# Decode states of an SSD mixer: GpSimd multiplies by C, VectorE only sums

## The chip, the cores and the metric

The kernel runs on one core of a Trainium2 chip. The metric is device time in microseconds (us): the median over executions. The stretch that matters here lies between 120 and 236 us of a profiled execution of 605.8 us.

## What is computed

One layer of a hybrid decoder, in float32, for 256 prompt rows and 8 decode rows (one new token for each of 8 sequences). After one input projection, one half of the columns feeds a gated convolution of 31 taps, the other a state-space block (SSD) with 16 heads in 4 groups. Then come an output projection, a mixture of 16 experts in 4 groups, a gate and a last norm. The part that changes is the SSD step of the 8 decode rows:

```
def step(h, inp):                      # for the prompt, in 2 chunks of 128 rows
    dec, st = inp
    return dec[..., None, None] * h + st, h
...
h_t = exp(dt_t A) h_{t-1} + dt_t x_t B_t^T        # for each decode row: state 64 x 128 in each head
y_t = h_t C_t                                     # sum over the 128 columns of the state
y = y + d_skip[:, None] * xs
y = y * silu(z)
```

and the decode rows' own convolutions: `causal_dwconv` of 31 taps over 30 kept rows and the new one, and one of 4 taps over x, B and C.

## The kernel before

Tensors lie with features on the 128 partitions. `T` is 264 columns: 256 prompt columns and 8 decode columns. Each engine has its own program in order; semaphores join them.

TensorE (`pe`) projects 40 blocks of 128 columns through `project(n)`, 32 of them before the SSD part. Then it transposes x, B and the decode rows' B and C (`bc_psum`), and runs 8 items, `item(i)`: two chunks times four groups. After each item one more projection stands (the last two convolutions by matmul, `c6` and `c7`, and blocks of z). An item needs `m_ready` from VectorE: the decay matrix `mexp` times `cbm`.

VectorE's loop over the 8 items does, for item i: `difference(i + 1)` (4 `tensor_scalar`, L1366), `spread_done(i)` (L1330, and in the second chunk L1335 and L1336), `take(i)` (it takes the item's result out of PSUM: L1346, or L1349 and L1350, and L1353 twice), and from i = 2 on `decode(i - 2)`. Behind item 1 it also runs `decode_conv()`, the 31-tap convolution of the decode rows (L1245 multiplies 1984 columns, L1248 sums them, L1250 adds the bias).

The decode state has 8 pieces of 128 partitions x 8 rows x 128 columns (1024 columns). For piece i:

- ScalarE, `decode(i)`: 8 activations scale the old state in place (L686), 8 more make `outer`, that is dt x times B (L691). B lies spread over all partitions in `bbc`, two groups at a time, C in `cbc`.
- GpSimd, `new_states(i)`: adds the two (L464), stores the new state to HBM (L470), for some pieces loads a later old state into a free place (L469). Behind pieces 1 and 3 it issues the DMA that spreads the next group of B (`spread_b`, L507), behind pieces 4 and 6 that of C (`spread_c`, L511), since `cbc` comes free when VectorE has read it.
- VectorE, `decode(i)`: 8 instructions `tensor_tensor_reduce` (L1378 in the profile, each with a read of its accumulator) multiply the new state by C and sum; then one small `scalar_tensor_tensor` (L1383) adds d_skip times x and sets `y_s_ready`.

ScalarE's loop for item i: `exp_of(i + 1)`, `exp_carry(i + 1)` in the second chunk (L667, which waits for item i to be done), a spread, `decode(i)`, and the evacuation of the projection behind the item. Ahead of piece 6 it also runs Silu over z (L727).

After the loop VectorE multiplies y by z for four groups (`gate_y`, L1409): three of them, then `decode(6)`, `decode(7)`, and the last one. The output projection (L989) needs all four and the norm behind them. It is followed by the experts, whose weights stream from HBM.

The spreads of B and C may start once `bbc`'s place is free. That place is `glu`, which the SP queue reads in 64 DMAs (L369, 16 for each of the four convolutions by matmul).

Of the kernel before, what the change touches and what calls it, by code (L numbers as in the profile page):

```python
# [83 lines left out]
def build(nc, xT, pT, w_in, w_dt, w_out, w_moe, w_router, b_router, w_pleg, w_ple, params, hparams,  # L84
          conf_s, ssm_s, state_s, yT, conf_p_out, ssm_p_out, h_p_out, conf_s_out, ssm_s_out, h_s_out):
    with ExitStack() as ctx:
# [42 lines left out]
        outer = scratch[:, 8192:10240].rearrange("p (q b n) -> p q b n", q=2, b=NSM)  # L129
# [113 lines left out]
        ln_rs = sem("ln_rs")  # L243
# [28 lines left out]
        snew_ready = sem("snew_ready")  # L272
        y_s_ready = sem("y_s_ready")
# [3 lines left out]
        grs = sem("grs")  # L277
# [4 lines left out]
        out_conf, out_ssm, out_h_p, out_h_s, out_y = [sem("out_" + n) for n in ("conf", "ssm", "h_p", "h_s", "y")]  # L282
# [36 lines left out]
        z_ready = sem("z_ready")  # L319
# [16 lines left out]
        def _(sp):  # L336
# [47 lines left out]
            for j in range(MOER):  # L384
                s = MOE_SLOT[j]
                if s < MIXR:
                    read(last_user[s])
                elif s == 3:
                    sp.wait_ge(proj_ready, POS["c", 7, 0] + 1)
                elif s >= 9:  # L390
                    sp.wait_ge(ycat_ready, NG)
                    sp.wait_ge(out_conf, 32)
                    sp.wait_ge(y_s_ready, KD)
                elif s == 8:
                    sp.wait_ge(snew_ready, KD)
# [33 lines left out]
            for s, n in ((out_conf, 2), (out_ssm, 2), (out_h_p, 1), (out_h_s, KD)):  # L429
                sp.wait_ge(s, 16 * n)  # L430
# [3 lines left out]
        def _(pool):  # L434
# [49 lines left out]
            for j in range(KD):  # L484
# [95 lines left out]
        def _(act):  # L580
# [98 lines left out]
            def decode(i):  # L679
# [32 lines left out]
            act.wait_ge(bc_psum, 1)  # L712
            a.activation(bc_keep, ps[0:64, 2, 0:P], ACT.Copy).then_inc(rows_kept, 1)
            exp_of(0)
            spread(2)
            for i in range(2 * NG):
# [6 lines left out]
                if i == 6:  # L723
# [3 lines left out]
                    a.activation(z0, z0, ACT.Silu).then_inc(z_ready, 1)  # L727
# [104 lines left out]
        def _(pe):  # L832
# [99 lines left out]
            for c in range(2):  # L932
                if c == 1:
                    pe.wait_ge(xconv_done, NX // 2)
                for hf in range(2):
# [5 lines left out]
                    ins.then_inc(xtok_psum, 1)  # L941
            project(NFIRST + 2)
# [230 lines left out]
        def _(dve):  # L1173
# [131 lines left out]
            decode_conv_x()  # L1305

# [4 lines left out]
            dve.wait_ge(out_ssm, 32)  # L1311
# [58 lines left out]
            def decode(i):  # L1370

                dve.wait_ge(snew_ready, i + 1)
                dve.wait_ge(c_loaded[i // 2 % 2], 16 * (i // 4 + 1))
                at = [0, 0]
                for b in range(NSM):
                    if b > 1:
                        dve.wait_ge(dve_self, at[b % 2])
                    at[b % 2] = mark(v.tensor_tensor_reduce(  # L1378
                        out=pr_s[:, 256 + P * (b % 2):256 + P * (b % 2 + 1)], in0=state[:, i % STATES, b, :],
                        in1=cbc[:, i // 2 % 2, b, :], scale=1.0, scalar=0.0, op0=ALU.mult, op1=ALU.add,  # L1380
                        accum_out=cat[:, 8 + i, NPR + b:NPR + b + 1]))
                dve.wait_ge(dve_self, at[1])
# [8 lines left out]
            for i in range(2 * NG):  # L1391
# [6 lines left out]
                if i == 0:  # L1398
                    dve.wait_ge(out_ssm, 32)
                if i == 1:  # L1400
                    decode_conv()
# [11 lines left out]
            dve.wait_ge(z_ready, 1)  # L1413
# [283 lines left out]
```

## Time and profile before

| | us |
|---|---|
| median of 3 runs | 608.87 (606.99 to 611.69) |
| profiled execution, its own time | 607.55 |
| its span, first to last instruction | 605.8 |
| TensorE busy in the span | 542.8 (90%) |
| VectorE busy | 266.5 (44%) |
| ScalarE busy | 162.4 (27%) |
| GpSimd busy | 87.6 (14%) |

The span is the time from the first to the last instruction that the profiler recorded; the execution's own time is 1.75 us longer. Busy shares are means over stages with very different limits. From 175 to 213 us, the last six items, VectorE is busy 27.02 of 38 us, ScalarE 32.37, TensorE 30.36 and GpSimd 18.56.

### The profile page before, as it was taken

What the parts mean: (1) busy time and instruction counts of PE and PEld (TensorE: products, weight loads), DVE (VectorE), ACT (ScalarE), POOL (GpSimd) and SP (SyncE); (2) the same over time, 40 slices, a digit from 0 to 9 for tenths busy, and PEclk for the clock granted to TensorE, in tenths of its full rate; (3) what the DMA queues carried; (4) which work ended last, traced back from release to release, by engine and by line L of the source; (5) the groups of instructions that cost most, each with busy time, mean ns of one, the idle gap of its engine ahead of it and who ended that gap; (6) DMA issues with size and microseconds to landing.
All of it is one profiled execution on the core that took longest, in us unless ns stands there. A gap on an engine that the chain in (4) does not pass through costs nothing.

```text
span 605.8 us, 7656 instructions
## 1 busy us (share of the span) xinstructions
PE 542.8 (90%) x2743; PEld 350.4 (58%) x2743; DVE 266.5 (44%) x783; ACT 162.4 (27%) x381; POOL 87.6 (14%) x104
## 2 busy tenths in 40 slices
PE   5999999999757877999976899999999999999994
PEld 3788888877525665888762344434343434343782
DVE  1799789413587676102271040404040404040553
ACT  3211311132488783312241101010101111111543
POOL 4000166123144440030000000000000000000000
PEclk9999999999869887999997899999999999999997
DMA  8733444449767860277972999999999999999101
GB/s 340 248 139 141 143 153 163 136 52 268 226 222 251 281 225 27 83 257 294 425 288 72 413 400 398 423 419 422 422 421 421 422 420 421 420 422 421 70 0 71
DMA packets 35609, 164.18 MB, mean 271 GB/s; under 512 B 6440, under 2 KB 12920, under 8 KB 19200
## 3 DMA queue, kind: packets, MB, share of 16 engines
q1 hardware_dynamic: 24960, 139.69, 58.8%
q0 software_dynamic: 6080, 21.80, 10.3%
q10 hardware_dynamic: 4544, 2.37, 1.5%
q8 instruction: 14, 0.23, 0.2%
q14 instruction: 11, 0.09, 0.0%
HBM read 153.43 MB, written 8.26 MB: 267 GB/s over the span
## 4 chain that ended last, share of the span: by engine, by line
PE 64%; DMA 16%; DVE 8%; issue 4%; SPq 3%; ACT 3%; POOL 2%; POOLq 0%; DVEq 0%; ACTq 0%
PE ps L889 14%; DMA xbc<-u_rows,slot_tok 12%; PE ps L989 10%; PE ps L1138 10%; PE ps L1109 10%; PE ps L1164 5%; PE ps L1152 4%; SPq L369 3%; PE ps L1075 2%; DVE xraw_s L1378 2%; DMA ring<-glu 2%; POOL glu L489 2%; PE ps L880 1%; DVE mexp L1366 1%; DMA ring<-bc_rows 1%
## 5 line engine op out<-in xcount | busy, mean ns | idle before, releaser
L889 PE MATMUL ps<-u,ring 128*128 128x264 f32 x640 | 144.7, 388 | 0.9 <-issue 0.9
L889 PEld LDWEIGHTS ps<-u,ring 128*128 128x128 f32 x640 | 122.1, 191 | 22.5 <-issue 1.6
L1109 PE MATMUL ps<-ring,xraw 128*64 128x512 f32 x512 | 114.9, 601 | 1.2 <-ACT xraw L792 1.2
L1109 PEld LDWEIGHTS ps<-ring,xraw 128*64 128x64 f32 x512 | 35.7, 138 | 69.2 <-issue 69.0
L1583 DVE TENSOR_TENSOR h<-h,ps 128x264 f32<-128x264 f32 x64 | 27.5, 429 | 86.0 <-PE ps L1152 85.2
L989 PE MATMUL ps<-cat,ring 128*128 128x264 f32 x256 | 59.5, 395 | 1.6 <-DVE cat L1428 1.6
L1138 PE MATMUL ps<-ring,xraw 128*64 128x512 f32 x256 | 58.6, 611 | 0.0
L989 PEld LDWEIGHTS ps<-cat,ring 128*128 128x128 f32 x256 | 49.7, 195 | 11.5 <-issue 2.7
L563 POOL DMA_INDIRECT xbc<-u_rows,slot_tok x9 | 8.6, 954 | 271.1 <-DVE slot_tok L1542 219.8
L1138 PEld LDWEIGHTS ps<-ring,xraw 128*64 128x64 f32 x256 | 18.1, 141 | 35.1 <-issue 35.1
L489 POOL TENSOR_TENSOR glu<-asg 128x256 f32<-128x256 f32 x8 | 21.4, 2671 | 94.7 <-ACT asg L637 94.7
L1152 PE MATMUL ps<-glu,xraw 128*128 128x264 f32 x128 | 30.6, 392 | 0.0
L1577 DVE TENSOR_TENSOR xraw<-xraw,ps 128x512 f32<-128x512 f32 x8 | 5.5, 688 | 55.7 <-PE ps L1109 55.7
L1164 PE MATMUL ps<-u,ring 128*128 128x264 f32 x128 | 28.9, 387 | 0.8 <-ACT u L812 0.8
L1152 PEld LDWEIGHTS ps<-glu,xraw 128*128 128x128 f32 x128 | 23.2, 188 | 10.6 <-issue 6.5
L1290 DVE SCALAR_TENSOR_TENSOR cat<-glu,prm,cat 128x256 f32<-128x256 f32 x60 | 28.3, 472 | 0.0
L1164 PEld LDWEIGHTS ps<-u,ring 128*128 128x128 f32 x128 | 24.2, 190 | 5.3 <-issue 1.2
L1290 DVE SCALAR_TENSOR_TENSOR prod<-glu,prm,prod 128x256 f32<-128x256 f32 x56 | 26.4, 472 | 0.0
L799 ACT ACTIVATE xraw<-ps 128x512 f32<-128x512 f32 x8 | 4.8, 597 | 80.0 <-PE ps L1109 80.0
L801 ACT ACTIVATE xraw<-ps 128x512 f32<-128x512 f32 x8 | 4.8, 597 | 70.8 <-PE ps L1123 70.8
L1075 PE MATMUL ps<-ident,xbc 128*128 128x128 f32 x72 | 12.1, 322 | 12.8 <-DMA xbc<-u_rows,slot_tok 12.8
L464 POOL TENSOR_TENSOR ring<-ring 128x1024 f32<-128x1024 f32 x8 | 19.1, 2388 | 26.2 <-ACT ring L691 20.8
(271 smaller groups left out, 591.7 us busy)
## 6 DMA issues: line engine op xcount, KB each, us to landing
ring<-in_w_moe SPq DMA_DIRECT2D x96, 1024.0 KB, 13.7
ring<-in_w_in SPq DMA_DIRECT2D x20, 1024.0 KB, 5.1
ring<-in_w_out SPq DMA_DIRECT2D x8, 1024.0 KB, 5.6
ring<-in_state_s POOLq DMA_DIRECT2D x8, 512.0 KB, 9.7
out_h_s_out<-ring POOLq DMA_DIRECT2D x8, 512.0 KB, 5.6
ring<-in_w_pleg SPq DMA_DIRECT2D x4, 1024.0 KB, 20.0
asg<-acs_rows ACTq DMA_DIRECT2D x8, 256.0 KB, 5.2
glu<-bc_rows POOLq DMA_DIRECT2D x4, 512.0 KB, 6.1
```

The costliest lines, as they stand in the source:

```text
L369: sp.dma_start(x4[32 * g:32 * g + 32, q % 2, i, 0:n], glu[32 * i:32 * i + 32, j, 8 * g:8 * g + n])\
L464: g.tensor_tensor(at, at, outer[:, i % 2], ALU.add).then_inc(snew_ready, 1)
L489: g.tensor_tensor(glu[:, j, KC - 1:], asg[:, 0, j % 2, 0:NPR], asg[:, 1, j % 2, 0:NPR], ALU.mult)
L889: ins = mm(ps[:, BANK[n], 0:T], wv[:, k, q * P:(q + 1) * P], u[:, k, :], start=(k == 0), stop=(k == KD - 1))
L989: ins = mm(ps[:, n, 0:T], wv[:, k, (n % 2) * P:(n % 2 + 1) * P], cat[:, 8 * (1 - hf) + k, :], start=(hf == 0 and k == 0), stop=(hf == 1 an ...
L1075: ins = tr(ps[:, 5 + c // 4, (c % 4) * P:(c % 4 + 1) * P], xgt[:, c * P:(c + 1) * P], ident[:, :])
L1109: ins = mm(ps[e * CAP:(e + 1) * CAP, gu, :], xg[:, 4 * hf + k, e * CAP:(e + 1) * CAP], wv[:, k, :], start=(hf == 0 and k == 0), stop=(hf = ...
L1138: ins = mm(ps[e * CAP:(e + 1) * CAP, 3 + o, :], hidt[:, 2 * hf + k, e * CAP:(e + 1) * CAP], wv[:, k, o * 512:(o + 1) * 512], start=(hf == ...
L1152: mm(ps[:, SC[q], 0:T], ysb[:, c, :], selt, start=True, stop=True).then_inc(sc_psum[q], 1)
L1164: ins = mm(ps[:, j % 4, 0:T], wv[:, k, (j % 2) * P:(j % 2 + 1) * P], u[:, k, :], start=(k == 0), stop=(k == KD - 1))
L1290: ins = v.scalar_tensor_tensor(out=acc, in0=src, scalar=w, in1=acc, op0=ALU.mult, op1=ALU.add)
L1583: v.tensor_tensor(h[:, c, :], h[:, c, :], ps[:, SC[q], 0:T], ALU.add).then_inc(sc_added[q], 1)
```

## The change

1. GpSimd, after the store of a new state, multiplies that state by C into the buffer of `outer` that it has just added from (`sc_ready`). VectorE's `decode(i)` is then one `tensor_reduce` over 1024 columns to 8, and the small d_skip instruction as before.
2. `outer` has three buffers in place of two. ScalarE's `outer` of piece i waits for `y_s_ready` of piece i - 3, no longer for GpSimd's addition of piece i - 2.
3. `spread_b` and `spread_c` of a group are issued together behind pieces 1 and 3, once the multiplication is done. The two waits of GpSimd for VectorE (`y_s_ready`, at `spread_c` and at the load of a later state) go.
4. `decode_conv()` moves from behind item 1 to a place ahead of the loop, right behind the small decode convolution.
5. The transposition of the decode rows' B and C, and ScalarE's copy of it, move ahead of two projections (to PSUM bank 7).
6. The stores of the last raw rows get a semaphore each, and VectorE waits for the small one alone.

```diff
-        outer = scratch[:, 8192:10240].rearrange("p (q b n) -> p q b n", q=2, b=NSM)
+        outer = [scratch[:, at:at + 1024].rearrange("p (b n) -> p b n", b=NSM) for at in (8192, 9216, 6200)]
...
                 at = state[:, i % STATES]
-                g.tensor_tensor(at, at, outer[:, i % 2], ALU.add).then_inc(snew_ready, 1)
+                g.tensor_tensor(at, at, outer[i % 3], ALU.add).then_inc(snew_ready, 1)
                 pool.wait_ge(snew_ready, i + 1)
                 if 2 <= i < STATES + 2:
                     pool.wait_ge(out_h_s, 16 * i)
-                    pool.wait_ge(y_s_ready, i - 1)
                     pool.dma_start(state[:, i - 2], state_s[:, STATES + i - 2]).then_inc(in_st[i - 2], 16)
                 pool.dma_start(h_s_out[:, i], at).then_inc(out_h_s, 16)
+                pool.wait_ge(c_loaded[i // 2 % 2], 16 * (i // 4 + 1))
+                g.tensor_tensor(outer[i % 3], at, cbc[:, i // 2 % 2], ALU.mult).then_inc(sc_ready, 1)
...
                 if i in (1, 3):
+                    pool.wait_ge(sc_ready, i + 1)
                     spread_b(i // 2 + 2)
-                if i in (4, 6):
-                    pool.wait_ge(y_s_ready, i - 2)
-                    spread_c(i // 2)
+                    spread_c(i // 2 + 2)
...
-                if i >= 2:
-                    act.wait_ge(snew_ready, i - 1)
+                if i == 2:
+                    act.wait_ge(conv_s_done, 1)
+                if i >= 3:
+                    act.wait_ge(y_s_ready, i - 2)
...
+                if n == NFIRST + 1:
+                    act.wait_ge(bc_psum, 1)
+                    a.activation(bc_keep, ps[0:64, 7, 0:P], ACT.Copy).then_inc(rows_kept, 1)
...
             decode_conv_x()
+            decode_conv()
...
-            dve.wait_ge(out_ssm, 32)
+            dve.wait_ge(out_ssm_p, 16)
...
-                dve.wait_ge(snew_ready, i + 1)
-                dve.wait_ge(c_loaded[i // 2 % 2], 16 * (i // 4 + 1))
-                at = [0, 0]
-                for b in range(NSM):
-                    if b > 1:
-                        dve.wait_ge(dve_self, at[b % 2])
-                    at[b % 2] = mark(v.tensor_tensor_reduce(
-                        out=pr_s[:, 256 + P * (b % 2):256 + P * (b % 2 + 1)], in0=state[:, i % STATES, b, :],
-                        in1=cbc[:, i // 2 % 2, b, :], scale=1.0, scalar=0.0, op0=ALU.mult, op1=ALU.add,
-                        accum_out=cat[:, 8 + i, NPR + b:NPR + b + 1]))
-                dve.wait_ge(dve_self, at[1])
+                dve.wait_ge(sc_ready, i + 1)
+                link(v.tensor_reduce(cat[:, 8 + i, NPR:T], outer[i % 3], AX.X, ALU.add))
```

GpSimd's program at pieces 3 and 4, before (`ring` holds state, `outer` and `cbc`; `glu` holds `bbc`):

```order
L464 TENSOR_TENSOR ring<-ring 128x1024 [waits outer_ready]
L469 DMA ring<-in_state_s 128x1024 [waits y_s_ready,out_h_s,snew_ready]
L470 DMA out_h_s_out<-ring 128x1024
L507 DMA glu<-bc_rows 128x1024
L464 TENSOR_TENSOR ring<-ring 128x1024 [waits outer_ready]
L469 DMA ring<-in_state_s 128x1024 [waits y_s_ready,out_h_s,snew_ready]
L470 DMA out_h_s_out<-ring 128x1024
L511 DMA ring<-bc_rows 128x1024 [waits y_s_ready]
```

and the same place now (the addition is line 463 here, the multiplication line 470):

```order
L463 TENSOR_TENSOR ring<-ring 128x1024 [waits outer_ready]
L467 DMA ring<-in_state_s 128x1024 [waits out_h_s,snew_ready]
L468 DMA out_h_s_out<-ring 128x1024
L470 TENSOR_TENSOR ring<-ring 128x1024 [waits c_loaded1]
L507 DMA glu<-bc_rows 128x1024 [waits sc_ready]
L511 DMA ring<-bc_rows 128x1024
L463 TENSOR_TENSOR ring<-ring 128x1024 [waits outer_ready]
L467 DMA ring<-in_state_s 128x1024 [waits out_h_s,snew_ready]
L468 DMA out_h_s_out<-ring 128x1024
L470 TENSOR_TENSOR ring<-ring 128x1024 [waits c_loaded0]
```

Each piece now has two additions or multiplications of 1024 columns in place of one, and both spreads stand behind piece 3.

VectorE's program from item 1's end to the first piece of decode, before:

```order
L1353 SCALAR_TENSOR_TENSOR cat<-xbc,prm,ps 128x128 x2
L1245 TENSOR_TENSOR ring<-ring,prm 128x1984 [waits glu_ready]
L1248 TENSOR_REDUCE cat<-ring 128x8x8 [waits dve_self]
L1250 TENSOR_TENSOR cat<-cat,prm 128x8x8 [waits dve_self]
L1366 TENSOR_SCALAR mexp<-asg,htok 128x128 [waits y_psum,acs_loaded1]
L1366 TENSOR_SCALAR mexp<-asg,htok 128x128 x3
L1330 TENSOR_TENSOR mexp<-mexp,cbm 128x512 [waits exp_ready]
L1346 COPY hst<-ps 128x256 [waits y_psum]
L1353 SCALAR_TENSOR_TENSOR cat<-xbc,prm,ps 128x128 x2
L1378 ISA xraw_s,cat<-ring 128x128 [waits c_loaded0,snew_ready]
```

and now (lines 1369, 1333, 1349 and 1356 are the old 1366, 1330, 1346 and 1353):

```order
L1356 SCALAR_TENSOR_TENSOR cat<-xbc,prm,ps 128x128 x2
L1369 TENSOR_SCALAR mexp<-asg,htok 128x128 [waits y_psum,acs_loaded1]
L1369 TENSOR_SCALAR mexp<-asg,htok 128x128 x3
L1333 TENSOR_TENSOR mexp<-mexp,cbm 128x512 [waits exp_ready]
L1349 COPY hst<-ps 128x256 [waits y_psum]
L1356 SCALAR_TENSOR_TENSOR cat<-xbc,prm,ps 128x128 x2
L1376 TENSOR_REDUCE cat<-ring 128x8 [waits sc_ready]
L1377 SCALAR_TENSOR_TENSOR cat<-xbc,prm,cat 128x8 [waits dve_self]
L1369 TENSOR_SCALAR mexp<-asg,htok 128x128 [waits y_psum,acs_loaded0]
```

The three instructions of `decode_conv` have left this place, and one reduction that waits for GpSimd's multiplication stands where the eight pairs of L1378 began.

## Rows read from the trace of the kernel before

**Rows 1.** The chain that ended last, in order of time: start us, us, what.

```profile
219.27 7.17 DMA ring<-bc_rows
...
230.62 0.72 DVE cat L1409
```

**Rows 2.** ScalarE, in order of time: first piece, an exponential, end of the loop.

```profile
169.29 0.40 ACT L691 ACTIVATE ring<-glu,dtx 128x128 f32<-128x128 f32 x1 [10.27 <-DMA glu<-bc_rows]
...
172.00 0.61 ACT L661 ACTIVATE mexp<-mexp 128x512 f32<-128x512 f32 x1
...
207.76 0.63 ACT L667 ACTIVATE ea<-asg 128x512 f32<-128x512 f32 x1 [1.34 <-PE ps L911]
...
218.41 2.43 ACT L691 ACTIVATE ring<-glu,dtx 128x128 f32<-128x128 f32 x8
```

**Rows 3.** Who waited for whom: us in total, times, longest us.

```profile
POOL glu L507 <- DMA ring<-glu: 10.4, 1, 10.4
```

**Rows 4.** TensorE, in order of time: first matmuls of items 2, 3, 4, 6 and 7.

```profile
175.03 1.12 PE L908 MATMUL ps<-mexp,xraw 128*64 128x128 f32 x8 [7.08 <-DVE mexp L1330]
...
177.24 5.58 PE L880 MATMUL ps<-ring 128*32 128x256 f32 x64
183.09 0.66 PE L908 MATMUL ps<-mexp,xraw 128*64 128x128 f32 x8 [0.26 <-DVE mexp L1330]
...
189.60 0.45 PE L908 MATMUL ps<-mexp,xraw 128*64 128x128 f32 x4 [1.67 <-DVE mexp L1330]
...
205.98 0.45 PE L908 MATMUL ps<-mexp,xraw 128*64 128x128 f32 x4 [1.40 <-DVE mexp L1330]
...
212.82 0.45 PE L908 MATMUL ps<-mexp,xraw 128*64 128x128 f32 x4 [1.53 <-DVE mexp L1330]
```

**Rows 5.** GpSimd, in order of time: multiplications, additions and a store.

```profile
74.94 7.82 POOL L489 TENSOR_TENSOR glu<-asg 128x256 f32<-128x256 f32 x1 [4.95 <-ACT asg L637]
...
140.78 1.91 POOL L478 TENSOR_TENSOR ring<-ea,fold 128x1024 f32<-128x1024 f32 x1 [1.59 <-PE ps L880]
...
171.82 2.47 POOL L464 TENSOR_TENSOR ring<-ring 128x1024 f32<-128x1024 f32 x1 [4.47 <-ACT ring L691]
174.59 0.56 POOL L470 DMA_DIRECT2D out_h_s_out<-ring  x1 [0.30 <-POOL ring L464]
...
189.77 2.36 POOL L464 TENSOR_TENSOR ring<-ring 128x1024 f32<-128x1024 f32 x1 [3.12 <-ACT ring L691]
```

**Rows 6.** VectorE, in order of time, ahead of the loop and around those additions.

```profile
144.47 4.88 DVE L1318 TENSOR_TENSOR xraw<-ps,htok 128x512 f32<-128x512 f32 x8 [11.12 <-DMA out_ssm_s_out<-xraw_s]
...
167.54 3.70 DVE L1248 TENSOR_REDUCE cat<-ring 128x64 f32<-128x1984 f32 x1
...
171.42 2.96 DVE L1366 TENSOR_SCALAR mexp<-asg,htok 128x128 f32<-128x128 f32 x4
...
185.27 0.28 DVE L1378 CUSTOM_DVE_ANT_0 xraw_s<-ring 128x128 f32<-128x128 f32 x1
...
187.22 0.87 DVE L1366 TENSOR_SCALAR mexp<-asg,htok 128x128 f32<-128x128 f32 x4
...
188.81 0.69 DVE L1336 TENSOR_TENSOR ea<-ea,xbc 128x512 f32<-128x512 f32 x1
191.38 1.03 DVE L1349 TENSOR_TENSOR hst<-hst,cdec 128x256 f32<-128x256 f32 x1 [1.88 <-PE ps L911]
...
195.12 0.23 DVE L1383 SCALAR_TENSOR_TENSOR cat<-xbc,prm,cat 128x8 f32<-128x8 f32 x1
...
200.33 0.43 DVE L1349 TENSOR_TENSOR hst<-hst,cdec 128x256 f32<-128x256 f32 x1 [2.79 <-PE ps L911]
```

**Rows 7.** Groups by line, engine and operation: count, busy us, mean ns, idle before.

```profile
L464 POOL TENSOR_TENSOR ring<-ring 128x1024 f32<-128x1024 f32 x8 | 19.1, 2388 | 26.2 <-ACT ring L691 20.8 <-DMA out_h_s_out<-ring 5.4
...
L1496 DVE TENSOR_REDUCE mexp<-mexp 128x6 f32<-128x96 f32 x1 | 0.3, 255 | 0.0
...
L1509 DVE TENSOR_REDUCE mexp<-mexp 128x6 f32<-128x24 f32 x1 | 0.2, 180 | 0.0
```

More of the change, by code:

```diff
@@ L242, in build @@
         ln_sq = sem("ln_sq")
-        ln_rs = sem("ln_rs")
         ln_n = sem("ln_n")
@@ L272, in build @@
         snew_ready = sem("snew_ready")
+        sc_ready = sem("sc_ready")
         y_s_ready = sem("y_s_ready")
@@ L276, in build @@
         gstat = sem("gstat")
-        grs = sem("grs")
         m_out_ready = sem("m_out_ready")
@@ L281, in build @@
         o_added = sem("o_added")
-        out_conf, out_ssm, out_h_p, out_h_s, out_y = [sem("out_" + n) for n in ("conf", "ssm", "h_p", "h_s", "y")]
+        out_conf, out_ssm_p, out_ssm_s, out_h_p, out_h_s, out_y = [sem("out_" + n) for n in
+            ("conf", "ssm_p", "ssm_s", "h_p", "h_s", "y")]
         wr_ready = sem("wr_ready")
@@ L318, in build @@
         x4_loaded = [sem(f"x4_loaded{q}") for q in range(2)]
-        z_ready = sem("z_ready")
         g_root = sem("g_root")
@@ L394, in _ @@
                 elif s == 8:
-                    sp.wait_ge(snew_ready, KD)
+                    sp.wait_ge(y_s_ready, KD)
                 else:
@@ L428, in _ @@
             sp.wait_ge(out_y, 16 * KD // 2)
-            for s, n in ((out_conf, 2), (out_ssm, 2), (out_h_p, 1), (out_h_s, KD)):
+            for s, n in ((out_conf, 2), (out_ssm_p, 1), (out_ssm_s, 1), (out_h_p, 1), (out_h_s, KD)):
                 sp.wait_ge(s, 16 * n)
@@ L496, in _ @@
                     pool.wait_ge(proj_evac, POS["x", 7, 1] + 1)
-                    pool.dma_start(ssm_p_out, xraw[:, :, NPR:]).then_inc(out_ssm, 16)
-                    pool.dma_start(ssm_s_out, xraw_s[:, :, 1:, :]).then_inc(out_ssm, 16)
+                    pool.dma_start(ssm_p_out, xraw[:, :, NPR:]).then_inc(out_ssm_p, 16)
+                    pool.dma_start(ssm_s_out, xraw_s[:, :, 1:, :]).then_inc(out_ssm_s, 16)
             make_taps(2)
@@ L687, in decode @@
                 act.wait_ge(b_loaded[i // 2 % 2], 16 * (i // 4 + 1))
-                if i >= 2:
-                    act.wait_ge(snew_ready, i - 1)
+                if i == 2:
+                    act.wait_ge(conv_s_done, 1)
+                if i >= 3:
+                    act.wait_ge(y_s_ready, i - 2)
                 for b in range(NSM):
-                    ins = a.activation(outer[:, i % 2, b, :], bbc[:, i // 2 % 2, b, :], ACT.Copy, scale=dtx[:, i, b:b + 1])
+                    ins = a.activation(outer[i % 3][:, b, :], bbc[:, i // 2 % 2, b, :], ACT.Copy, scale=dtx[:, i, b:b + 1])
                 ins.then_inc(outer_ready, 1)
@@ L711, in _ @@
                     .then_inc(btok_ready, 1)
-            act.wait_ge(bc_psum, 1)
-            a.activation(bc_keep, ps[0:64, 2, 0:P], ACT.Copy).then_inc(rows_kept, 1)
             exp_of(0)
@@ L726, in _ @@
                     z0 = zs[:, 0:6, :]
-                    a.activation(z0, z0, ACT.Silu).then_inc(z_ready, 1)
+                    a.activation(z0, z0, ACT.Silu)
                 decode(i)
@@ L941, in _ @@
                     ins.then_inc(xtok_psum, 1)
+            pe.wait_ge(xbc_ready, NX // 2 + 1)
+            pe.wait_ge(htok_ready, 1)
+            tr(ps[0:64, 7, 0:P], bc_cols, ident[:, :]).then_inc(bc_psum, 1)
             project(NFIRST + 2)
@@ L947, in _ @@
                 if c == 1:
-                    pe.wait_ge(htok_ready, 1)
+                    pe.wait_ge(rows_kept, 1)
                 for gr in range(NG):
@@ L958, in _ @@
                 ins.then_inc(cb_psum, 1)
-            pe.wait_ge(xbc_ready, NX // 2 + 1)
-            tr(ps[0:64, 2, 0:P], bc_cols, ident[:, :]).then_inc(bc_psum, 1)
             for i in range(2 * NG):
@@ L1397, in _ @@
                 take(i)
[L1398 to L1401, printed above, removed]
                 if i >= 2:
@@ L1412, in _ @@
             dve.wait_ge(proj_evac, NSEQ)
-            dve.wait_ge(z_ready, 1)
             dve.wait_ge(y_ready, 2 * NG)
```

## The prediction

> **What bounds the kernel now.** I read the chain that ended last first. In the stretch of the change it ends in the last spread of C (issued at 219.27, 7.17 us) and the last `gate_y` at 230.62 [rows 1]. Behind that, the output projection and the experts' weights follow in order, so a shift of the last `gate_y` moves the end one for one. The sum is the shift of that one instruction.
>
> Second, ScalarE: its first `outer` starts at 169.29, after 10.27 us of waiting for the first spread of B [rows 2]. That spread itself waits 10.4 us for SP's DMAs that read `glu` [rows 3]; the change touches neither. Third, TensorE: items 2, 3, 4, 6 and 7 start at 175.03, 183.09, 189.60, 205.98 and 212.82, the last three after waits of 1.4 to 1.7 us for VectorE [rows 4]. So from item 4 on VectorE's cycle of some 8 us sets the pace. Item 3 waits 0.26 us only, since the projection before it ends at 177.24 + 5.58 = 182.82 [rows 4].
>
> Fourth, VectorE and GpSimd side by side. Four L1366 take 0.87 us alone and 2.96 us at 171.42, ending at 174.38, where GpSimd's addition runs from 171.82 to 174.29. L1349 (two SBUF inputs) takes 0.43 us alone and 1.03 us at 191.38, where an addition runs until 192.13 [rows 5, 6]. Turned round, GpSimd's multiplication of 256 columns at 74.94 takes 7.82 us beside VectorE's back-to-back convolution, though 1024 columns take 2.39 us in the mean elsewhere [rows 5, 7]. One excludes the other for a whole instruction.
>
> **The change, part by part.** The moves ahead of the loop give nothing that I can place. `decode_conv` leaves VectorE behind item 1 (its reduction alone is 3.70 us, at 167.54) and goes into the 11.12 us in which VectorE waited until 144.47 for the stores of the raw rows [rows 6]. With its multiplication it is some 6 us, so it fits. What it leaves behind is no gain at once: item 2 needs ScalarE's exponential, which stands behind the first `outer` and ends at 172.61 [rows 2], and L1330 then meets the addition that runs until 174.29 [rows 5], 0.7 us before item 2, as it did. The earlier B and C rows and the narrower wait for the raw rows are covered by SP's DMAs in the same way; without that cover they would be worth up to the 10.4 us of [rows 3]. So items 2 and 3 start at 175.0 and 183.1 as before.
>
> In the loop, VectorE's decode took 1.95 us (185.27 to 187.22 [rows 6]). The new one is a reduction of 1024 contiguous columns. From 24 to 96 columns at 6 results a reduction grows by 75 ns, 1.04 ns for each column [rows 7]: 0.16 + 1.06 = 1.2 us, plus 0.2 for the small L1383 that stays: 1.4 us, 0.55 less for each of eight pieces. The other bound is the strided reduction, 3.70 us for 1984 columns [rows 6], 1.9 us for 1024, and then nothing is saved. I take 1.2, as the small rows are contiguous like the new one.
>
> GpSimd gets eight multiplications. None with these operands is in the trace. The nearest are 1.91 us for a multiplication of 1024 columns whose inputs repeat [rows 5] and 2.39 for the addition with the same shape and two full inputs [rows 7]; I take 2.39. Each follows its addition by 0.9 us (0.30 wait and 0.56 store issue [rows 5]), 1.45 where a state load is issued too.
>
> What these do to VectorE decides. In a cycle of the second chunk, L1366, L1330, L1335 and L1336 take 187.22 to 189.50, 2.3 us, L1349 0.43 and L1383 0.23: 3.0 us in which it must exclude GpSimd, if what [rows 5, 6] show holds for all that read two SBUF inputs. GpSimd now needs 2 x 2.39 = 4.8, together 7.8 of a cycle of 8. VectorE leaves two gaps: its wait for TensorE (1.88 us [rows 6]), and the work on PSUM (some 0.9) with the reduction (1.2). Each is shorter than 2.39, so every GpSimd instruction, wherever it falls, holds VectorE up by 0.3 to 0.5 us at least and by 2.4 at most. Before there was one for each cycle, and it started within 0.3 us of L1336's end (189.77 against 189.50), in the first gap.
>
> I walked the engines through the loop with these durations. Item 4: the multiplication of piece 1 waits for L1330 and runs 181.65 to 184.05; the two spreads take until 185.4; the addition of piece 2 runs 185.45 to 187.85 and holds L1383 (ready at 186.5); the differences and L1330 end at 189.5, 0.8 later than before. The multiplication of piece 2 takes the port there and holds L1336 until 191.9. Item 4 starts at 192.8 instead of 189.60. Item 5: addition 3 runs 192.8 to 195.2 and holds L1349, multiplication 3 runs 196.65 to 199.05 and holds L1383, addition 4 takes the port at 200.7 and holds L1336 until 203.1. Items 6 and 7 keep the loss: 212.1 and 220.0 instead of 205.98 and 212.82.
>
> The tail gives some back: decode 6 waited for C until 226.44, and now C is there. ScalarE's last `outer` ended at 220.84, 13.1 us behind the L667 of 207.76 [rows 2]; that L667 is now near 213.9, so the last `outer` is at 227.0. Behind it come the first three `gate_y`, the addition, its store, the multiplication (233.2 to 235.6), the reduction and L1383: the last `gate_y` near 237.0, +6.4. The same walk through the instructions of before ends at 231.6, 1.0 late, so I take that off: **+5.4 us**, 607.55 + 5.4 = 613.0 against the profiled execution. With 1.91 for a multiplication, five collisions are 0.5 shorter and it is +3. That execution is 1.3 under the median of 3, inside their scatter (606.99 to 611.69); I carry half of this: **613.5**.
>
> The Trainium skill, page "SBUF — State Buffer", section "Who interferes with whom", says that VectorE and GpSimd share one port pair as an exclusive lock, held for the full instruction by whichever starts first, and that a `tensor_reduce` on VectorE never contends. By that rule, the trace agrees on the lock [rows 5, 6]; no row of before shows a reduction beside GpSimd work. If the reduction were held up as well, the forecast would lie by up to 2 us an item higher.
>
> **The rivals.** First, the gaps align (faster). If every GpSimd instruction fell where VectorE does not need the port, items 4 to 7 would each gain 0.55 us, 2.2 in all, and the end would no longer wait for the spread of C: last `outer` at 218.7, GpSimd's backlog 0.8, addition 2.39, store 0.9, multiplication 2.39, decode 1.4, so the last `gate_y` at 226.6, 4.0 us early: 603.6, or 604.2 with the same half carried. For it: before, the additions did fall into such a gap. Against it: both gaps are shorter than 2.39 us, and the multiplication starts 3.3 to 3.8 us behind the addition's start, when VectorE reaches L1383.
>
> Second, a draw. If the collisions cost 0.3 to 0.5 us each, always at a gap's start, they eat the 0.55 us of each decode, and the tail's gain of 1.6 stands against one or two large collisions: 606.5 to 609.5. The change then does on VectorE what it says, and the time doesn't move.
>
> Third, GpSimd becomes the bound (slower by over 1%). A piece on GpSimd is 2.39 + 0.9 + 2.39 = 5.7 us, 6.2 with a load and 7.3 with the two spreads. Where VectorE holds the port, GpSimd starves as in the row of 7.82 us [rows 5]. If its two instructions wait more than about 2 us an item, y lags behind `outer`, whose buffer waits for piece i - 3; every cycle is then near 10 us, five of them 10 to 12 us late: 618 to 620.
>
> **How the numbers follow.** The forecast's case, 609.5 to 618, gets 0.55; the aligned gaps 0.17; the draw 0.20; GpSimd as the bound 0.08. The range runs from 604.0 to 618.0: it leaves out the bound GpSimd and about half of the aligned gaps. This kernel's measurement tells about 1% (6.1 us) from no change, so slower begins at 614.96. Of the forecast's case some 0.22 lies above that, with the third rival 0.30. Faster by over 1% needs more than 6 us, and the aligned gaps give 4.0, more only if the waits for TensorE shrink too: 0.07. The rest, 0.63, is within 1%.
>
> **What would show it.** Right: items 2 and 3 near 175.0 and 183.1; items 4 to 7 later by 3 to 7 us; L1336, L1349 or L1383 with spans of 1 to 2.5 us that end with a GpSimd instruction; the reduction at 1.2 us whether or not GpSimd is busy; no wait for C at decode 6; the last `gate_y` 4 to 7 us later. Wrong: items 4 to 7 earlier than before, and GpSimd's instructions longer than 2.5 us, that is, waiting in VectorE's place. It would also be wrong if the first spread of B came earlier than about 165 us, which I hold to be fixed by SP, or if GpSimd multiplied in far less than 1.9 us.

## The result and the profile after

The changed kernel takes 617.62 us (median of 4 runs, 616.98 to 619.09) beside 607.93 us of the kernel before on the same chip (605.82 to 611.69). The ratio is 1.0157, with a 95% interval of 1.0106 to 1.0208: slower by over 1%. The forecast was 613.5 in a range of 604 to 618. So the direction holds, and the range by 0.4 us only: the loss is +9.7 us where the walk through the profile gave +5.4.

The profiled execution took 617.47 us, its span is 615.7 us, 9.9 more than before. The last `gate_y` (now L1399) starts at 240.57 instead of 230.62 [rows 1], 9.95 later, and 375.1 us follow it (375.2 before). The whole loss lies ahead of that instruction. (Of the profiles told of below, that of the kernel without multiplication is of a disturbed execution, 3 us above its median, so its stages serve for the loop alone.) In the changed kernel L1333, L1338, L1339, L1352, L1353, L1369 and L1377 are the old L1330, L1335, L1336, L1349, L1350, L1366 and L1383; L1376 is the new reduction.

TensorE of the changed kernel, in order of time, the first matmuls of items 2 to 7 (start us, us, engine, line, operation, in brackets the idle time before it):

```profile
174.87 1.12 PE L910 MATMUL ps<-mexp,xraw 128*64 128x128 f32 x8 [5.25 <-DVE mexp L1333]
...
183.88 0.66 PE L910 MATMUL ps<-mexp,xraw 128*64 128x128 f32 x8 [1.64 <-DVE mexp L1333]
...
194.81 0.70 PE L910 MATMUL ps<-mexp,xraw 128*64 128x128 f32 x4 [6.08 <-DVE mexp L1333]
...
207.28 0.55 PE L910 MATMUL ps<-mexp,xraw 128*64 128x128 f32 x4 [4.37 <-issue]
...
215.39 0.45 PE L910 MATMUL ps<-mexp,xraw 128*64 128x128 f32 x4 [1.18 <-DVE mexp L1333]
...
223.39 0.45 PE L910 MATMUL ps<-mexp,xraw 128*64 128x128 f32 x4 [2.70 <-DVE mexp L1333]
```

Against [rows 4], item 2 starts 0.2 us earlier, item 3 0.8 later, item 4 5.2, item 6 9.4 and item 7 10.6 later. Item 5 is 9.6 later; before, it was this row:

```profile
197.64 0.45 PE L908 MATMUL ps<-mexp,xraw 128*64 128x128 f32 x4 [2.74 <-DVE mexp L1330]
```

So the loss comes between items 2 and 5, nearly all in the two steps to items 4 and 5.

VectorE of the changed kernel, in order of time:

```profile
132.30 2.23 DVE L1247 TENSOR_TENSOR ring<-ring,prm 128x1984 f32<-128x1984 f32 x1 [9.47 <-POOL ring L490]
...
179.81 3.42 DVE L1369 TENSOR_SCALAR mexp<-asg,htok 128x128 f32<-128x128 f32 x4
...
186.06 1.21 DVE L1376 TENSOR_REDUCE cat<-ring 128x8 f32<-128x1024 f32 x1
...
187.45 5.84 DVE L1369 TENSOR_SCALAR mexp<-asg,htok 128x128 f32<-128x128 f32 x4
...
193.82 0.16 DVE L1338 COPY cdec<-ea 128x4 f32<-128x4 f32 x1
...
197.99 2.32 DVE L1352 TENSOR_TENSOR hst<-hst,cdec 128x256 f32<-128x256 f32 x1 [3.29 <-PE ps L913]
...
204.12 2.33 DVE L1338 COPY cdec<-ea 128x4 f32<-128x4 f32 x1
...
217.17 1.16 DVE L1352 TENSOR_TENSOR hst<-hst,cdec 128x256 f32<-128x256 f32 x1 [1.88 <-PE ps L913]
...
219.21 1.21 DVE L1376 TENSOR_REDUCE cat<-ring 128x8 f32<-128x1024 f32 x1
...
230.16 3.18 DVE L1377 SCALAR_TENSOR_TENSOR cat<-xbc,prm,cat 128x8 f32<-128x8 f32 x1
233.26 4.50 DVE L1399 TENSOR_TENSOR cat<-cat,ring 128x528 f32<-128x528 f32 x3
...
240.57 0.71 DVE L1399 TENSOR_TENSOR cat<-cat,ring 128x528 f32<-128x528 f32 x1
```

GpSimd of the changed kernel beside it: L463 is the addition, L470 the multiplication, L467 the load of a later state.

```profile
171.92 2.34 POOL L463 TENSOR_TENSOR ring<-ring 128x1024 f32<-128x1024 f32 x1 [6.34 <-ACT ring L692]
...
175.15 2.37 POOL L470 TENSOR_TENSOR ring<-ring 128x1024 f32<-128x1024 f32 x1
...
180.75 2.38 POOL L470 TENSOR_TENSOR ring<-ring 128x1024 f32<-128x1024 f32 x1
...
188.36 2.35 POOL L470 TENSOR_TENSOR ring<-ring 128x1024 f32<-128x1024 f32 x1
190.67 2.34 POOL L463 TENSOR_TENSOR ring<-ring 128x1024 f32<-128x1024 f32 x1
196.51 0.59 POOL L467 DMA_DIRECT2D ring<-in_state_s  x1 [3.51 <-DMA out_h_s_out<-ring]
...
197.66 2.36 POOL L470 TENSOR_TENSOR ring<-ring 128x1024 f32<-128x1024 f32 x1
...
203.98 2.45 POOL L463 TENSOR_TENSOR ring<-ring 128x1024 f32<-128x1024 f32 x1 [2.54 <-ACT ring L692]
...
219.48 2.37 POOL L470 TENSOR_TENSOR ring<-ring 128x1024 f32<-128x1024 f32 x1
...
228.64 2.36 POOL L470 TENSOR_TENSOR ring<-ring 128x1024 f32<-128x1024 f32 x1
230.95 2.35 POOL L463 TENSOR_TENSOR ring<-ring 128x1024 f32<-128x1024 f32 x1
...
234.19 2.36 POOL L470 TENSOR_TENSOR ring<-ring 128x1024 f32<-128x1024 f32 x1
```

The two are read together by their ends. Four differences take 0.87 us alone [rows 6]. At 187.45 they take 5.84: multiplication 2 starts at 188.36, addition 3 follows it without a gap at 190.67 and ends at 193.01, and only then do they go on. (The one of the four that is held, the third, starts at 187.84 by the record, while GpSimd still issues the store ahead of multiplication 2. It takes 0.27 us alone; why it did not finish first stays open, as for the row at 195.75 in the kernel with own stores below.) The copy L1338 takes 0.16 us alone and 2.33 at 204.12, until addition 4 ends at 206.43. L1352 takes 2.32 at 197.99, until multiplication 3 ends at 200.02. The pattern stands once more at 230.16: a small instruction of 0.23 us waits 2.95 us for the rest of multiplication 6 and the whole of addition 7. The reduction takes 1.21 us at 219.21, although multiplication 5 runs from 219.48: it is not held.

ScalarE of the changed kernel, in order of time: first `outer`, last `exp_carry`, last `outer`.

```profile
169.39 0.40 ACT L692 ACTIVATE ring<-glu,dtx 128x128 f32<-128x128 f32 x1 [9.92 <-DMA glu<-bc_rows]
...
217.17 0.63 ACT L666 ACTIVATE ea<-asg 128x512 f32<-128x512 f32 x1 [0.77 <-PE ps L913]
...
227.82 2.43 ACT L692 ACTIVATE ring<-glu,dtx 128x128 f32<-128x128 f32 x8
```

Against [rows 2] the first `outer` starts 0.1 us later and both of the others 9.4 us later. ScalarE follows the items; it doesn't set them.

GpSimd's waits in the same kernel (us in total, times, longest us):

```profile
POOL glu L507 <- DMA ring<-glu: 18.2, 1, 18.2
...
POOL ring L467 <- DMA out_h_s_out<-ring: 3.5, 1, 3.5
```

The first is the wait of [rows 3], longer because GpSimd comes to it earlier. It ends 1.8 us earlier than before, but ScalarE's first `outer` isn't earlier. The second is new: the load of a later state waits until the stores of all earlier pieces have landed.

### The profile page after: what moved, and what is told of

It reads as the page before. It is cut to its first block, busy times and chain, and to the rows that moved or that the text cites. A ratio compares the mean times of both kernels' runs of the same rounds, so it can differ in the third digit from the quotient of the medians.

```text
span 615.7 us, 7537 instructions
## 1 busy us (share of the span) xinstructions
PE 546.8 (89%) x2743; PEld 353.2 (57%) x2743; DVE 277.2 (45%) x663; ACT 162.8 (26%) x381; POOL 106.4 (17%) x112
## 4 chain that ended last, share of the span: by engine, by line
PE 61%; DMA 16%; DVE 9%; SPq 5%; issue 4%; ACT 2%; POOL 2%; POOLq 0%; DVEq 0%; ACTq 0%
PE ps L891 14%; DMA xbc<-u_rows,slot_tok 12%; PE ps L991 10%; PE ps L1111 9%; PE ps L1140 9%; PE ps L1166 5%; SPq L368 4%; PE ps L1154 4%; DMA ring<-glu 2%; PE ps L1077 2%; DVE mexp L1369 2%; POOL glu L489 1%; DVE cat L1376 1%; PE ps L1071 1%; DVE hst L1352 1%
## 5 line engine op out<-in xcount | busy, mean ns | idle before, releaser
L891 PE MATMUL ps<-u,ring 128*128 128x264 f32 x640 | 147.0, 392 | 0.0
L891 PEld LDWEIGHTS ps<-u,ring 128*128 128x128 f32 x640 | 124.0, 194 | 22.4 <-issue 0.4
L910 PE MATMUL ps<-mexp,xraw 128*64 128x128 f32 x64 | 8.0, 352 | 24.4 <-DVE mexp L1333 20.1
L1166 PE MATMUL ps<-u,ring 128*128 128x264 f32 x128 | 28.9, 387 | 0.8 <-ACT u L814 0.8
L1154 PEld LDWEIGHTS ps<-glu,xraw 128*128 128x128 f32 x128 | 23.2, 188 | 10.6 <-issue 6.5
L1166 PEld LDWEIGHTS ps<-u,ring 128*128 128x128 f32 x128 | 24.2, 190 | 5.3 <-issue 1.2
## 6 DMA issues: line engine op xcount, KB each, us to landing
ring<-in_w_moe SPq DMA_DIRECT2D x96, 1024.0 KB, 14.5
```

Source lines behind the costliest of these rows:

```text
L891: ins = mm(ps[:, BANK[n], 0:T], wv[:, k, q * P:(q + 1) * P], u[:, k, :], start=(k == 0), stop=(k == KD - 1))
L1154: mm(ps[:, SC[q], 0:T], ysb[:, c, :], selt, start=True, stop=True).then_inc(sc_psum[q], 1)
L1166: ins = mm(ps[:, j % 4, 0:T], wv[:, k, (j % 2) * P:(j % 2 + 1) * P], u[:, k, :], start=(k == 0), stop=(k == KD - 1))
```

## The experiments

Three theories were on trial. **A**: VectorE's instructions with two SBUF inputs and its `tensor_scalar` and copies wait while GpSimd works on SBUF, and these holds lie on the path from item to item. **B**: the sums come late, because GpSimd has more to do, and the time follows GpSimd's length. **C**: the moves (decode convolution, B and C rows, spreads) cost or bring the time.

One table holds all kernels. "Loop" is from item 2's first matmul to item 7's, "end" from there to the last `gate_y`, "rest" from there to the end of the span; these, and item 2, are from the profiled run. "Held" is the sum, over VectorE's instructions between items 2 and 7, of what they took beyond their length alone, counted where it is over 0.3 us; five pieces of decode lie in that stretch. Ratios are against runs of the kernel before on the same chip; its medians there were 607.93, 608.58, 607.93 and 607.27 us.

| kernel | median us | ratio | item 2 | loop | held | end | rest |
|---|---|---|---|---|---|---|---|
| before | 607.93 | | 175.03 | 37.79 | 2.02 | 17.80 | 375.2 |
| changed | 617.62 | 1.0157 [1.0106, 1.0208] | 174.87 | 48.52 | 13.92 | 17.18 | 375.1 |
| no multiplication | 606.87 | 0.9939 [0.9887, 0.9990] | 174.08 | 38.47 | 4.82 | 17.23 | 378.5 |
| fill instead | 611.47 | 1.0070 [1.0030, 1.0109] | 175.55 | 44.49 | 9.74 | 15.83 | 374.8 |
| moves alone | 608.84 | 1.0017 [0.9973, 1.0061] | 174.07 | 40.50 | 2.46 | 14.36 | 377.9 |
| multiplications alone | 614.76 | 1.0117 [1.0042, 1.0193] | 180.43 | 41.60 | 8.39 | 17.26 | 376.1 |
| gap | 620.21 | 1.0185 [1.0101, 1.0270] | 176.28 | 46.04 | 12.65 | 17.14 | 381.2 |
| held back | 614.08 | 1.0091 [1.0041, 1.0140] | 176.02 | 39.90 | 5.32 | 19.74 | 378.2 |
| own stores | 625.72 | 1.0290 [1.0189, 1.0391] | 176.64 | 52.42 | 17.62 | 19.12 | 376.0 |
| held back, own stores | 610.67 | 1.0040 [1.0000, 1.0080] | 176.89 | 39.93 | 5.37 | 18.60 | 374.4 |
| last two on VectorE | 615.94 | 1.0142 [1.0073, 1.0211] | 176.22 | 47.63 | 12.56 | 16.55 | 373.2 |
| all three | 608.73 | 1.0006 [0.9972, 1.0040] | 176.19 | 39.97 | 4.83 | 15.59 | 376.8 |

The rest, the experts' stage, differs by up to 8 us among kernels whose code there is the same; single profiles don't settle differences of a few us in the total.

The table's reading is the strongest result here: for the ten kernels in which VectorE only sums in the loop, the loop less the held time is 33.2 to 35.1 us, while the held time runs from 4.8 to 17.6. Before, it is 35.8, and 2.0 us are held: 0.61 at 191.38 [rows 6] and 1.41 in this first of eight instructions that take 0.28 alone, beside an addition:

```profile
178.20 1.69 DVE L1378 CUSTOM_DVE_ANT_0 xraw_s<-ring 128x128 f32<-128x128 f32 x1
```

The loop's loss of 10.7 us then adds up: 11.9 more held, 2.8 less for five decodes (1.39 us each, from 186.06 to 187.45, where it was 1.95 [rows 6]), and 1.7 more for TensorE's lower clock (below). The moves alone are the exception, 38.0: VectorE waits 2.42 us for the last but one spread of C there, at 211.01.

**No multiplication** (the changed kernel without GpSimd's multiplication):

```diff
-                g.tensor_tensor(outer[i % 3], at, cbc[:, i // 2 % 2], ALU.mult).then_inc(sc_ready, 1)
...
-                dve.wait_ge(sc_ready, i + 1)
+                dve.wait_ge(snew_ready, i + 1)
```

> The changed kernel with GpSimd's multiplication left out: VectorE sums the outer product dt x B instead of state times C, right behind GpSimd's addition (that part of the computation is missing). Everything else stands as changed. Theory A (GpSimd's multiplications exclude VectorE's instructions while they run): 603 to 606, items 4 to 7 earlier than before the change. Theory C (the moves of the decode convolution and of the B and C rows, or the new waits of ScalarE, cost the time): 614 to 618.

606.87 us, 10.75 below the changed kernel; the loop is 38.47 us. That is 0.9 above A's range and far from C's: the multiplications are the loss. What they cost, held instructions or lateness, this run alone doesn't tell.

**Fill instead of multiplication** (GpSimd is busy for 1.72 us a piece, where a multiplication takes 2.36, and reads nothing):

```diff
-                g.tensor_tensor(outer[i % 3], at, cbc[:, i // 2 % 2], ALU.mult).then_inc(sc_ready, 1)
+                at, step = ((7224, 968), (7224, 1992), (6200, 1024))[i % 3]
+                pool.wait_ge(conv_s_done, 1)
+                pool.wait_ge(sc_ready, i)
+                g.memset(scratch[:, at:at + 2 * step].rearrange("p (a n) -> p a n", a=2)[:, :, 0:960], 0.0)\
+                    .then_inc(sc_ready, 1)
```

> The changed kernel with each multiplication replaced by a GpSimd fill of 1920 columns, which reads nothing and keeps GpSimd busy for an estimated 1.7 us (0.83 us for 855 columns in the profile); VectorE sums what it finds in the buffer (the product with C is missing). The sums wait for the fill as they do for the multiplication. Theory A in the form of the port's read side (only a GpSimd instruction that reads holds two-input VectorE instructions): 604 to 609; the tensor_scalar and copies may still be held. Theory B (the sums come too late, since they wait for addition, store and multiplication in a row, and ScalarE waits for the sums): 614 to 617, a little under the changed kernel.

611.47 us, between the two expectations: by the ratios about half of the loss. Part of that is the shorter instruction. VectorE of this kernel, in order of time (L1373 is the difference, L1356 the old L1349):

```profile
187.49 2.82 DVE L1373 TENSOR_SCALAR mexp<-asg,htok 128x128 f32<-128x128 f32 x4
...
197.15 0.42 DVE L1356 TENSOR_TENSOR hst<-hst,cdec 128x256 f32<-128x256 f32 x1 [3.29 <-PE ps L917]
```

and GpSimd's fills at the same places:

```profile
188.25 1.72 POOL L473 MEMSET ring<- 128x1920 f32 x1
...
196.87 1.72 POOL L473 MEMSET ring<- 128x1920 f32 x1
```

The differences wait for the fill (188.25 to 189.97), 1.96 us beyond their 0.86. The multiplication with two SBUF inputs, at 197.15, runs inside the other fill in its 0.42 us, where in the changed kernel it waited for a multiplication. What VectorE is held by depends on what GpSimd's instruction does, which lateness can't explain. The Trainium skill, page "SBUF — State Buffer", section "Who interferes with whom", states both halves: two SBUF inputs contend with a GpSimd instruction that reads SBUF and not with one that only writes it, `copy` and `tensor_scalar` in their two-port modes contend in any case. These two rows agree.

**Moves alone** (the changed kernel with the decode, the place of the spreads of C and GpSimd's and ScalarE's waits of before):

```diff
-                g.tensor_tensor(outer[i % 3], at, cbc[:, i // 2 % 2], ALU.mult).then_inc(sc_ready, 1)
...
                 if i in (1, 3):
-                    pool.wait_ge(sc_ready, i + 1)
                     spread_b(i // 2 + 2)
-                    spread_c(i // 2 + 2)
+                if i in (4, 6):
+                    pool.wait_ge(y_s_ready, i - 2)
+                    spread_c(i // 2)
```

> The changed kernel with the decode of before: VectorE multiplies and sums (eight pairs a piece), GpSimd only adds, the spreads of C and the loads wait for VectorE as before. The moves of the decode convolution, of the B and C rows and of the raw rows' waits, and the third outer buffer stay. Theory A: 606 to 609, as before the change. Theory C: 614 to 618.

608.84 us, no change that can be told. C falls: the moves neither cost nor bring in the total. In the profile the loop is 2.7 us longer, with the wait for C told of above, and the end 3.4 us shorter.

**Multiplications alone** (the kernel before with GpSimd's multiplication, three `outer`, the sums and the paired spreads):

```diff
                 pool.dma_start(h_s_out[:, i], at).then_inc(out_h_s, 16)
+                pool.wait_ge(c_loaded[i // 2 % 2], 16 * (i // 4 + 1))
+                g.tensor_tensor(outer[i % 3], at, cbc[:, i // 2 % 2], ALU.mult).then_inc(sc_ready, 1)
```

> The kernel before with the multiplications on GpSimd, VectorE's sums and the spreads in pairs; decode convolution, B and C rows and the waits for the raw rows stand where they were. Theory A: 614 to 620. Theory C: 606 to 610.

614.76 us, in A's range. Most of the loss is there without the moves. Here the worst hold comes one item earlier: the differences at 174.15 take 5.63 us, and item 2 starts at 180.43.

**Gap** (GpSimd waits for the end of each multiplication ahead of the next addition):

```diff
+                pool.wait_ge(sc_ready, i + 1)
```

> The changed kernel with one more wait: GpSimd waits for the end of each multiplication before it goes on to the next addition, so that a gap of some 0.3 us stands between the two. Theory A (a VectorE instruction with two inputs or a tensor_scalar waits while GpSimd works, and gets no turn between two GpSimd instructions that stand back to back): the difference at L1369 that took 5.84 us at 187.45 is let in behind multiplication 2 and takes about 3.4, item 3 comes 1 to 2.4 us earlier than 194.81, the same for the d_skip of 3.18 us at 230.16; the time is 613 to 616. Theory B (the sums come late because GpSimd has more to do, and the time follows GpSimd's length): six gaps of 0.3 us more on GpSimd, 618 to 620.

620.21 us: A's number failed, and the time is at the upper edge of what B expected. The mechanism is nevertheless seen at its place. VectorE of this kernel (L1339 copies `cdec`, L1340 is the multiplication of `ea`):

```profile
188.98 0.87 DVE L1370 TENSOR_SCALAR mexp<-asg,htok 128x128 f32<-128x128 f32 x4
...
190.36 2.33 DVE L1339 COPY cdec<-ea 128x4 f32<-128x4 f32 x1
192.72 0.69 DVE L1340 TENSOR_TENSOR ea<-ea,xbc 128x512 f32<-128x512 f32 x1
```

and GpSimd, multiplication 2 and addition 3:

```profile
190.14 2.52 POOL L470 TENSOR_TENSOR ring<-ring 128x1024 f32<-128x1024 f32 x1
192.74 2.88 POOL L463 TENSOR_TENSOR ring<-ring 128x1024 f32<-128x1024 f32 x1
```

The differences end at 189.85, ahead of multiplication 2, and escape it. The copy L1339 waits for that multiplication; given a gap, VectorE gets it and L1340 in, and it is now addition 3 that takes 2.88 us instead of 2.34. The step from item 3 to item 4 is 8.1 us, against 10.9 in the changed kernel. But the next pieces collide in its place (3.60 us for the differences at 198.19, 2.85 for L1339 at 202.31), and the loop is only 2.5 us shorter. The profiled run started item 2 1.4 us later and spent 6.1 us more in the experts' stage; why the total is no better stays open.

**Held back** (multiplications 0 to 5 start only when VectorE has issued the masking of the item two on, after which it waits for TensorE):

```diff
+                if i + 2 < NG:
+                    pool.wait_ge(m_ready, i + 3)
+                elif i + 2 < 2 * NG:
+                    pool.wait_ge(ce_ready, i + 3 - NG)
                 g.tensor_tensor(outer[i % 3], at, cbc[:, i // 2 % 2], ALU.mult).then_inc(sc_ready, 1)
```

> The changed kernel, whole in its work, with each of the multiplications 0 to 5 held back on GpSimd until VectorE has issued the masking of the item two on (the m or ce semaphore), after which VectorE waits for TensorE anyway. Theory A (held instructions of VectorE on the path from item to item are the loss): the differences, L1333 and L1338 stand outside the multiplications, items come 1.5 to 2 us apart less than in the changed kernel, and the time is 607 to 611. Theory B (lateness of the sums is the loss): multiplications come later still, so 618 to 622.

614.08 us, between the two expectations, and its interval overlaps that of the changed kernel. In the loop A is right: the same work, later on GpSimd, takes 39.90 us instead of 48.52. B, by which later multiplications lengthen the loop, falls. Of these 8.6 us, 1.8 are left in the span of the profiled execution (3.5 in the medians): item 2 comes 1.2 us later than in the changed kernel, the end is 2.6 us longer and the rest 3.1. VectorE there (L1373 the difference, L1356 the old L1349):

```profile
180.95 0.86 DVE L1373 TENSOR_SCALAR mexp<-asg,htok 128x128 f32<-128x128 f32 x4
...
217.70 4.69 DVE L1356 TENSOR_TENSOR hst<-hst,cdec 128x256 f32<-128x256 f32 x1 [1.88 <-PE ps L917]
```

and GpSimd, multiplication 5 and addition 6:

```profile
217.43 2.37 POOL L474 TENSOR_TENSOR ring<-ring 128x1024 f32<-128x1024 f32 x1
219.75 2.34 POOL L463 TENSOR_TENSOR ring<-ring 128x1024 f32<-128x1024 f32 x1
```

The differences behind item 2 are free (0.86 us, 3.42 in the changed kernel), since multiplication 1 waits for L1337 and starts at 182.57. Behind item 7, multiplication 5 and addition 6 stand back to back once more, and L1356 waits for both.

**Own stores** (a load waits for the stores of its own parity, which takes away the new wait of 3.51 us):

```diff
+        out_h_s = [out_h_s, sem("out_h_s1")]
...
-                    pool.wait_ge(out_h_s, 16 * i)
+                    pool.wait_ge(out_h_s[i % 2], 16 * (i // 2))
...
-                pool.dma_start(h_s_out[:, i], at).then_inc(out_h_s, 16)
+                pool.dma_start(h_s_out[:, i], at).then_inc(out_h_s[i % 2], 16)
...
```

> The changed kernel in which the load of a state waits only for the stores of its own parity, which takes away GpSimd's wait of 3.51 us at 196.51. Theory A: addition and multiplication 3 come 2 to 3 us earlier and hold other instructions of VectorE; only chance decides which, 616 to 619. Theory B (GpSimd's lateness): the pieces behind it come 3 us earlier, 613.5 to 615.

625.72 us, 8 us worse than the changed kernel: against both expectations, and the opposite of B's. VectorE (L1341 is the old L1336):

```profile
195.75 3.34 DVE L1341 TENSOR_TENSOR ea<-ea,xbc 128x512 f32<-128x512 f32 x1
```

GpSimd, multiplication 3:

```profile
196.18 2.35 POOL L472 TENSOR_TENSOR ring<-ring 128x1024 f32<-128x1024 f32 x1
```

Without the wait, multiplication 3 starts 1.4 us behind addition 3's end, when VectorE is amid its way to item 4, and holds one of its two-input instructions until 198.5. In the changed kernel the wait had kept GpSimd quiet from 193.0 to 196.5, while VectorE did exactly this. Held time 17.62, loop 52.42.

**Held back, own stores** (both edits):

> Both edits: multiplications held until VectorE has masked the item two on, and loads that wait only for stores of their own parity. Theory A: 606 to 611, within 1.5 us of the kernel with the held multiplications alone, since the wait for the stores then lies in GpSimd's slack. Theory B: 3 us below the kernel with the held multiplications alone.

610.67 us, in A's range, but 3.4 us below the kernel held back alone, which is B's number (3 us) and not A's (1.5 at most). The intervals of the two overlap, so the 3.4 us are not shown, and in the profiles 3.8 us of difference lie in the experts' stage. The loop is no shorter (39.93 against 39.90), so it isn't earlier sums. What the edit does change is the end, 1.1 us shorter: multiplication 5 now starts at 216.87, addition 6 only at 220.23, and the old L1349 at 218.61 takes 0.91 us instead of 4.69.

**Last two on VectorE** (the changed kernel; GpSimd multiplies pieces 0 to 5, VectorE treats 6 and 7 as before):

```diff
-                g.tensor_tensor(outer[i % 3], at, cbc[:, i // 2 % 2], ALU.mult).then_inc(sc_ready, 1)
+                if i < 6:
...
+                    g.tensor_tensor(outer[i % 3], at, cbc[:, i // 2 % 2], ALU.mult).then_inc(sc_ready, 1)
...
```

> The changed kernel in which GpSimd multiplies the pieces 0 to 5 only, and VectorE multiplies and sums the pieces 6 and 7 by the instructions of the kernel before. Theory A (behind the last item the three gates are held by GpSimd's last addition and multiplication, and the last sum waits for multiplication 7): from item 7 to the last gate 14 to 14.5 us instead of 17.2, the time 614 to 615.5; the loop from item 2 to item 7 stays at 48 to 49 us. Theory B (the last additions alone set that end): 16.5 to 17.5 us from item 7 to the last gate, 616.5 to 618.

615.94 us, between the two expectations, and the end is 16.55 us, which is B's number, not A's 14 to 14.5. The gates wait 2.79 us for ScalarE's last evacuation first and start at 232.52, so ScalarE's last pieces set the first 8.7 us of that end.

**All three** (held back, own stores, last two on VectorE):

> The same last two pieces on VectorE, with the multiplications 0 to 5 held until VectorE has masked the item two on and the loads waiting for stores of their own parity only. Theory A: the loop as in the kernel with both edits (39.9 us), the end 15 us instead of 18.6, so 606 to 608, no different from the kernel before. Theory B: 609.5 to 611.5.

608.73 us, no change against before that can be told, between A's 606 to 608 and B's 609.5 to 611.5; loop 39.97 and end 15.59 us. Six of the eight multiplications on GpSimd, placed where VectorE waits, cost nothing and bring nothing.

## Why the prediction was right in direction and short in size

- **Moves worth nothing:** right. Shown by the moves alone, and in the profile by `decode_conv` at 132.30 and items 2 and 3 at 174.87 and 183.88 (175.0 and 183.1 forecast).
- **Terms of the instructions:** right. The reduction takes 1.21 us (1.2), a multiplication 2.35 to 2.38 (2.39), and it follows its addition by 0.9 (174.26 to 175.15). "0.55 less" for each decode: 1.39 us instead of 1.95, 0.56 less.
- **Exclusion, and that the reduction escapes it:** right; the reduction took 1.21 us wherever it ran. But a GpSimd instruction need not cost "0.3 to 0.5 us at least": multiplication 4 (207.84 to 210.19) lies whole in VectorE's wait for TensorE, which ends at 210.31.
- **Item 4, the step that failed:** "The multiplication of piece 2 takes the port there and holds L1336 until 191.9", item 4 at 192.8. The walk let VectorE in between GpSimd's instructions and took a collision to cost "2.4 at most". In the run, addition 3 followed multiplication 2 without a gap, the four differences lost 4.97 us to the pair, and item 4 started at 194.81, with 0.8 of it lost ahead at item 3 (L1369 at 179.81). The rows at 230.16, and those of the kernel held back at 217.70, show the same; the gap kernel shows that a gap lets VectorE in.
- **Item 5:** forecast 11.2 us behind item 4, measured 12.5. Of the three collisions named, L1352 (the old L1349) was held, but by multiplication 3, and lost 1.9 us; addition 4 held the copy L1338 (2.2 us lost) and not the multiplication behind it; L1377 was not held. TensorE's clock took part: after idling 6.08 us ahead of item 4 it ran that item at 1.2 GHz, as the windows of items 4 and 6 of the changed kernel show (the last three columns are granted clock, DMA share and GB/s):

```profile
194.80:197.70 2.90, 2.90 (x18) 2.44 (x19) 0.00 (x0) 0.00 (x0) 1.17 (x3) 0.50 0.50 206
...
215.40:217.10 1.70, 1.70 (x19) 1.48 (x20) 0.00 (x0) 1.00 (x3) 1.41 (x1) 1.00 0.80 279
```

  At 0.50 VectorE waits 3.29 us for the item, at 1.00 it waits 1.88. Over items 4 to 6 these waits are 3.29, 3.12 and 1.88 us, before 1.88, 2.79 and 1.88 [rows 6 for the first two], so the clock gives 1.7 us of the loop's loss.
- **Items 6 and 7:** 8.1 and 8.0 us apart, as forecast. Item 7 came at 223.39, not 220.0: 3.4 us of the missing size. So the signs that were named failed in size: items 4 to 7 came 5.2 to 10.6 us later, not 3 to 7, and the last gate 9.95, not 4 to 7.
- **The end:** 17.18 us; the walk had 17.0. That they agree is partly luck. In the walk the gates stand ahead of the last addition, and multiplication 7 and the last sum set the end. In the run addition 7 came first, held L1377 at 230.16, and the three gates lost 2.6 us to multiplication 7 (4.50, against 1.94 in the kernel with the moves alone); they ended behind it, and both sums behind them. From the walk's end 1.0 was taken off, because the walk of before was 1.0 late. That correction was wrong here and is the other 1.0. No wait for C, as forecast.
- **Rivals:** the aligned gaps didn't come by themselves; held back by hand, the loop came near to its old length. GpSimd as the bound is near in time (618 to 620), but GpSimd isn't it: VectorE's waits in the loop are for TensorE, none is for a product.

## What to carry to other kernels

Moving work from VectorE to GpSimd is not priced by busy time: add up what VectorE's `tensor_scalar`, copies and two-input instructions on the path wait while GpSimd works, for up to a whole instruction each time, and for the whole run where two GpSimd instructions stand back to back. If such work must go to GpSimd, tie its start to a semaphore that says that VectorE has just begun to wait for another engine; here that gave back 8.6 of 10.7 us of the loop, though only 3.5 of 9.7 us of the time. A wait on GpSimd may be what keeps it out of VectorE's way, so look at what stands beside it before taking it away.

## What the runs showed of the hardware that was not expected

- A waiting VectorE instruction got no turn between two GpSimd instructions that followed each other without a gap: at 187.45, at 230.16 and, in the kernel held back, at 217.70 it lost 4.97, 2.95 and 4.27 us, where one multiplication or addition of GpSimd lasts 2.3 to 2.5.
- Beside an addition of GpSimd, VectorE ran free where it has one SBUF input only. In the kernel held back with own stores, VectorE (an addition from PSUM, L1359, two of L1362, whose `prm` is one number for each partition, and the reduction):

```profile
212.96 0.42 DVE L1359 TENSOR_TENSOR hst<-hst,ps 128x256 f32<-128x256 f32 x1
213.30 0.60 DVE L1362 SCALAR_TENSOR_TENSOR cat<-xbc,prm,ps 128x128 f32<-128x128 f32 x2
213.81 1.21 DVE L1382 TENSOR_REDUCE cat<-ring 128x8 f32<-128x1024 f32 x1
```

and GpSimd's addition 5 at the same time:

```profile
212.61 2.54 POOL L465 TENSOR_TENSOR ring<-ring 128x1024 f32<-128x1024 f32 x1
```

- A fill by GpSimd, which reads nothing, held four `tensor_scalar` (2.82 us instead of 0.86) and left a two-input instruction alone (0.42 us).
